# Routing head 0 of tile 0 as its own piece, with the order of TensorE, ScalarE and VectorE changed around the first row gathers

## What is computed

```python
h = h + concat([y_mla, y_diff]) @ w_out
# _peer, on n = rms_norm(h), in chunks of 128 tokens
q = (n @ w_query).reshape(128, 8, 2, 128)
s = einsum('chpd,hpnd->chpn', q, sub_keys)           # 8 heads, 2 halves, 128 keys each
s1, i1 = top_k(s[:, :, 0], 16); s2, i2 = top_k(s[:, :, 1], 16)
best, flat = top_k(all 256 sums of s1 and s2, 16)    # per head
experts = i1[flat // 16] * 128 + i2[flat % 16]       # 16 rows of 16384 for each head and token
g = softmax(best)
act = gelu(einsum('cd,chkd->chk', n, u[experts]))
h = h + einsum('chk,chkd->cd', g * act, v[experts])
```

## Time and profile before

| what | value |
| --- | --- |
| median of 3 runs | 1566.36 us |
| span of the profiled execution, first to last instruction | 1493.2 us |
| PE busy | 1221.3 us (82%) |
| DVE busy | 1039.1 us (70%) |
| POOL busy | 582.6 us (39%) |
| ACT busy | 425.9 us (29%) |
| DMA | 435.45 MB, mean 292 GB/s |

### The profile page before, as it was taken

How to read it: one execution, slowest core, us unless ns; L and a number is a source line. 1 busy time by engine, 2 the same in 40 slices (tenths; PEclk the granted TensorE clock), 3 DMA queues, 4 the chain that set the end, 5 groups by cost and what they waited for, 6 DMA issues and landing times.

```text
span 1493.2 us, 17594 instructions
## 1 busy us (share of the span) xinstructions
PE 1221.3 (82%) x6525; PEld 888.2 (59%) x6525; DVE 1039.1 (70%) x1903; ACT 425.9 (29%) x740; POOL 582.6 (39%) x644
## 2 busy tenths in 40 slices
PE   6997997677786565665566579999999999999997
PEld 3545675344443222222222229989989999899996
DVE  5786468888688775866666546677777759575655
ACT  1147213021112111211110114333345556243342
POOL 4140026777777777777777742001010000000000
PEclk9999898788998778777788899999999999999999
DMA  9917149999999999999999986888757545357651
GB/s 328 358 42 254 57 171 340 394 409 400 409 409 408 408 400 401 410 408 410 409 410 409 410 350 214 284 286 283 262 182 242 189 165 184 113 170 228 203 187 71
DMA packets 179708, 435.45 MB, mean 292 GB/s; under 512 B 13881, under 2 KB 84610, under 8 KB 179638
## 3 DMA queue, kind: packets, MB, share of 16 engines
q0 software_dynamic: 84384, 306.26, 52.3%
q1 hardware_dynamic: 94214, 126.18, 25.3%
q10 hardware_dynamic: 1040, 2.10, 0.4%
HBM read 433.44 MB, written 2.14 MB: 292 GB/s over the span
## 4 chain that ended last, share of the span: by engine, by line
PE 47%; POOL 28%; issue 10%; DVE 6%; DMA 5%; ACT 2%; SPq 0%; DVEq 0%; POOLq 0%
POOL arena L795 21%; PE quad L1505 14%; POOL ring L795 7%; PE quad_a L1610 7%; PE quad_a L1519 6%; PE quad_a L1204 4%; DMA ring<-in_ffn_w_gu_dram 3%; PE quad_a L1459 2%; PE quad_a L1305 2%; PE quad L1287 2%; DMA arena<-in_peer_v_dram,arena 2%; PE quad_a L1687 2%; PE quad_a L1675 2%; PE quad_a L1533 1%; ACT arena L823 1%
## 5 line engine op out<-in xcount | busy, mean ns | idle before, releaser
L1459 PE MATMUL quad_a<-arena 128*128 128x512 f32 x384 | 200.0, 685 | 124.0 <-DMA arena<-in_peer_v_dram,arena 124.0
L1459 PEld LDWEIGHTS quad_a<-arena 128*128 128x128 f32 x384 | 84.5, 225 | 238.9 <-issue 238.6
L795 POOL DMA_INDIRECT arena<-in_peer_v_dram,arena x193 | 186.0, 964 | 61.8 <-issue 58.0
L1505 PE MATMUL quad<-u_hi,w_hi 128*128 128x256 f32 x704 | 199.5, 283 | 0.6 <-DVE u_lo L2018 0.6
L1505 PE MATMUL quad<-u_lo,w_hi 128*128 128x256 f32 x704 | 199.2, 283 | 0.0
L1505 PE MATMUL quad<-u_hi,w_lo 128*128 128x256 f32 x704 | 199.0, 283 | 0.0
L795 POOL DMA_INDIRECT arena<-in_peer_u_dram,arena x168 | 170.9, 1017 | 58.7 <-issue 50.6
L722 POOL DMA_DIRECT2D arena<-in_w_ada_dram x60 | 31.8, 531 | 401.0 <-DVE arena L1753 398.8
L1976 DVE TENSOR_TENSOR w_lo<-ring,w_hi 128x2048 fp32r<-128x2048 f32 x66 | 150.7, 2289 | 52.2 <-ACT w_hi L994 52.0
L988 ACT ACTIVATE arena<-ident,arena 128x128 f32<-128x128 f32 x192 | 59.6, 389 | 343.4 <-DVE arena L2123 343.4
L2133 DVE SCALAR_TENSOR_TENSOR hx<-arena,hx 128x1024 f32<-128x1024 f32 x46 | 59.1, 1284 | 135.9 <-DMA arena<-in_peer_v_dram,arena 135.6
(11 more groups left out here) (374 smaller groups left out, 2415.0 us busy)
## 6 DMA issues: line engine op xcount, KB each, us to landing
ring<-in_ffn_w_gu_dram SPq DMA_DIRECT2D x44, 1024.0 KB, 9.1
arena<-in_w_ada_dram POOLq DMA_DIRECT2D x60, 512.0 KB, 6.3
ring<-in_ffn_w_down_dram SPq DMA_DIRECT2D x22, 1024.0 KB, 5.0
ring<-in_w_mix_in_dram SPq DMA_DIRECT2D x20, 1024.0 KB, 6.6
arena<-in_peer_w_query_dram SPq DMA_DIRECT2D x4, 2048.0 KB, 9.8
ring<-in_w_ada_dram POOLq DMA_DIRECT2D x12, 512.0 KB, 10.4
arena<-in_w_in_dram SPq DMA_DIRECT2D x3, 2048.0 KB, 35.7
arena<-in_w_out_dram SPq DMA_DIRECT2D x2, 2048.0 KB, 11.3
```

The lines of the kernel that those rows point to most:

```text
L795: gp.indirect_dma_start(out=rows_of(n), out_offset=None, in_=t["peer_" + kind][0], in_offset=bass.IndirectOffsetOnAxis(ap=expert[tt][:, sl ...
L1459: last = te.matmul(sum_side[tt][:, cols], diag[:, i % DIAGS], rows_of(n)[:, cols], start=(slot == pe_slots[0]), stop=(slot == pe_slots[-1] ...
L1505: last = te.matmul(psum[c][:, w * SEQ:(w + 1) * SEQ], weight[a][:, k, (c % 2) * P:(c % 2 + 1) * P], (u_hi, u_lo)[b][:, k], start=(k == 0 a ...
```

## The change

- `PIECES` splits the first piece: head 0 and head 1 are pieces 0 and 1 now. The first quarter of the queries is made, evacuated, scored and searched in two halves of two segments (`first_query`, `first_scores`, `evac_half`, `first_keys`). The second quarter moves behind tile 1's output projection, its `top_keys` into group 1 of DVE's loop, and piece 1's `pick` into group 0.
- `values(7)` on PE and its copy on DVE move behind the transposition of `hn`; the root of tile 1's attention norm moves behind the first half evacuation on ACT, and `y_turned(1)` behind the memsets on DVE.
- On ACT, gelu of group 0 stands ahead of the `ada` evacuations, and gelu of group 1 ahead of quarters 2 and 3. On PE, `query(0, 3)` and the scores of quarters 2 and 3 move behind the sums of group 0.
- The first two query tiles leave `ring`. A new tile `row8` is the buffer 8; the turn is 9 buffers at n = 0, a tenth at n = 9 (it waits for `hn_in_psum`), two more at n = 32, four at 128, four at 160: 20 in all, before 19.
- `NORM1_AT` and `QUERY1_AT` go from 1 and 2 to 2 and 3.

```diff
-        pq_at = [(ring, 0), (ring, 512), (arena, R0 + 7168), (arena, R0 + 7680)], ...
+        pq_at = [(arena, R0 + 10240), (arena, R0 + 5632), (arena, R0 + 7168), (arena, R0 + 7680)], ...
-        OPENED = {0: range(0, 11), 128: range(11, 15), 160: range(15, 19)}
+        OPENED = {0: (0, 1, 2, 3, 4, 5, 8, 6, 7), 9: (9,), 32: (10, 11), 128: range(12, 16), 160: range(16, 20)}
-        PIECES = ((0, 0, 2), (0, 2, 2), (0, 4, 4), (1, 0, 4), (1, 4, 4))
-        ROUTE_AT = {1: 1, 5: 2, 11: 3, 18: 4}
-        KEYS_AT = {3: (0, 2), 4: (0, 3), 9: (1, 0), 10: (1, 1), 14: (1, 2), 16: (1, 3)}
-        NORM1_AT, QUERY1_AT = 1, 2
+        PIECES = ((0, 0, 1), (0, 1, 1), (0, 2, 2), (0, 4, 4), (1, 0, 4), (1, 4, 4))
+        ROUTE_AT = {1: 2, 5: 3, 11: 4, 18: 5}
+        KEYS_AT = {1: (0, 1), 3: (0, 2), 4: (0, 3), 9: (1, 0), 11: (1, 1), 14: (1, 2), 16: (1, 3)}
+        NORM1_AT, QUERY1_AT = 2, 3
...
-            pool.wait_ge(a_full.sem, a_at["ps", 0, 1] + 1)
+            pool.wait_ge(a_full.sem, a_at["ps", 0, 0, 0] + 1)
...
-                elif 11 <= buffer_of[n] < 15:
+                elif 12 <= buffer_of[n] < 16:
                     pool.wait_ge(a_full.sem, a_at["pq", 1, 0] + 1)
-                elif buffer_of[n] >= 15:
+                elif buffer_of[n] >= 16:
                     pool.wait_ge(a_full.sem, a_at["pq", 1, 1] + 1)
...
+            evac_half("pq", 0)
             root(("subln", 1))
-            evac_query("pq", 0, 0)
-            evac_query("ps", 0, 0)
-            evac_query("pq", 0, 1)
-            spread_rows(0)
-            evac_query("ps", 0, 1)
-            soft(0)
-            for job in ADA_JOBS:
-                ...
+            for what, half in (("ps", 0), ("pq", 1), ("ps", 1)):
+                evac_half(what, half)
+            for piece in range(2):
+                spread_rows(piece)
+                soft(piece)
             sc_e.wait_ge(d_free.sem, len(d_jobs))
             hn_in_psum.mark(ac.activation(hn_side[0], hn[0], ACT.Copy))
-            for what, n in (("pq", 2), ("pq", 3), ("ps", 2), ("ps", 3)):
-                evac_query(what, 0, n)
+            for what in ("pq", "ps"):
+                evac_query(what, 0, 1)
...
             for group in range(QT * GROUPS):
                 gelu_group(group)
+                if group == 0:
+                    for job in ADA_JOBS:
+                        ...
+                if group == 1:
+                    for what, n in (("pq", 2), ("pq", 3), ("ps", 2), ("ps", 3)):
+                        evac_query(what, 0, n)
...
-            top_keys(0, 0)
+            first_keys(0)
             top_pairs(0)
             pick(0)
-            top_keys(0, 1)
+            first_keys(1)
+            top_pairs(1)
             for n in range(2):
                 written_out(n, 1)
             normalize(0)
-            ve.wait_ge(a_full.sem, a_at["ada", ADA_JOBS[-1]] + 1)
...
+                if group == 0:
+                    pick(1)
+                    normalize(1)
                 if group in KEYS_AT:
```

74 lines of the change are left out of this document (49 added, 25 removed).

## The result

The changed kernel takes 1587.38 us (median of 6, 1580.12 to 1588.69), the kernel before 1565.36 us beside it (median of 6, 1563.52 to 1570.63): ratio 1.0136, 95% interval 1.0118 to 1.0153. It is slower by 22 us; forecast was 1557. One thing must be known to read any number here: the trace of before with its span of 1493.2 us was taken where this kernel takes 1496 us, and the timed runs where it takes 1565; the experiments met both kinds of chip, and each is told with the time of the kernel before beside it.

What follows compares the result with a forecast made beforehand. It took the gathers to be paced by DMA bytes from about 270 us, the end set by gather 0's issue and early losses: 9.5 - 0.8 = 8.7, call it 9; 1566.4 - 9 = 1557 us, range 1548 to 1567.

Steps and rivals of the forecast that it cites:

- With the 73.2 us between span and median: Last step: 73.2 us between traced span and median time, carried through unchanged, so 1566.4 - 9 = 1557 us.
- PE doesn't stand in the way by then: Early gathers: PE's second and third quarters, `ada` and group 0 sums, done by 243, were not to delay POOL.
- Cost nothing; the cover is 5 us: n = 32 to 127: group 1's diagonals at 254.5, its first buffer wanted at 262.7; no loss.
- a further wait among n = 32 to 60: Sign against the forecast: another wait of POOL at these gathers would show it wrong; no size given.
- Slower: Rival, chance 0.08: PE at half clock holds group 1's `v` rows until 275, buffers over 15 us late; 1576 at 20 us delay.
- The clock: Cause in the slower rival: PE at 1.2 GHz makes 20 us of sums, query and scores take 40; rival's chance 0.08.
- The steps ahead of the first gather: Reordered and halved query, search and pick before gather 0: issued at 199.2 instead of 206.80, gain 7.6 us (6 to 11).
- The waits that come: POOL at n = 18 late by 3.7 us, some 2 absorbed, and at n = 29 late by 4.7 us, both behind DVE.
- Gather 30: End of the early waits: issued at 245.3 against 254.78 before, 9.5 us sooner.
- I take 0.4 at each: Buffers opened at n = 128 and 160 wait for tile 1 queries: 2.4 us late, mostly hidden, 0.4 us lost at each.
- the short routing instructions: DVE's two-operand routing among the gathers could hold up POOL, up to 5 us, 1562; rival's chance 0.04.

Runs made afterwards that it cites:

- `b_again`: The kernel before, unedited, run again: 1496.33 us, beside 1495.93 us for the kernel before (ratio 1.0005).
- `b_third`: The kernel before, unedited, run a third time: profiled run 1561.93 us, beside 1565.25 us for the kernel before.
- `a_again`: The changed kernel, unedited, run again: 1493.32 us, beside 1495.93 us for the kernel before (ratio 0.9989).
- `a_third`: The changed kernel, unedited, run a third time: 1582.65 us, beside 1565.25 us for the kernel before (ratio 1.0107).
- `e_open`: The changed kernel with new buffers joined at n = 132 and 164 instead of 128 and 160: 1573.87 us, kernel before 1565.25 (ratio 1.0056).
- `e_direct`: The changed kernel with each gather replaced by a plain transfer of 128 successive rows, same bytes: 1484.75 us, kernel before 1565.96 (ratio 0.9486).
- `e_fix`: `e_both` with ACT's evacuations of quarters 2 and 3 in group 2, behind gelu and tile 1's root: 1563.25 us, ratio 0.9975; run again 1565.40, 0.9995.
- `e_both`: `e_split` plus new buffers joined at n = 132 and 164: 1571.31 us, kernel before 1567.08 (ratio 1.0015).
- `e_split`: The changed kernel with ACT's quarter 2 and 3 evacuations behind group 1's diagonals and `query(0, 3)` in two halves: 1585.65 us, kernel before 1567.08 (ratio 1.0115).

## Why the prediction was wrong

**The failing step is the last of the sum: "With the 73.2 us between span and median".** I took 73.2 us for time around the span. In the executions here time and span lie 1.7 us apart (1588.69 and 1587.0 in the changed kernel's own, 1493.98 and 1492.3 in `b_again`). A span of 1493.2 beside a median of 1566.36 meant that the trace came from other conditions than the times, and that 68 us of waiting were missing from it (the spans of `b_third` and `b_again`, 1560.2 and 1492.3). Every price in the sum was read from a trace without them. What made the forecast's gain a loss is the next step.

**"PE doesn't stand in the way by then", and "Cost nothing; the cover is 5 us" for the diagonals of group 1.** Right for the earlier trace rows and for `a_again`; on the chips of the timed runs `query(0, 1)` and `query(0, 3)` take 20 and 17 us instead of 7.4, the diagonals come at 282 instead of 254.5, and the cover of 5 us is gone: 13.8 us at n = 44. That is the sign that the forecast named against itself, a further wait among n = 32 to 60. The rival "Slower" had this place and nearly this price ("v rows of group 1 held until 275", over 15 us late, 1576), with another cause. The clock is not it: at 247 to 267 the granted clock was 1.00 while PE ran dry. It fell at 207 to 227 (0.67) after PE had begun to run dry, and so is a part of the price, not its source: the 32 `ada` entries behind took 6.83 us in `a_third` for 4.68 in `a_again`.

**The steps ahead of the first gather** were right: 199.2 forecast, 197.58 in `a_again`, 199.73 in the changed kernel's trace; the gain is 8.3 us on one chip (`b_again` 205.92), forecast 7.6.

**The waits that come.** n = 18: 3.7 us late forecast, 5.3 measured (5.57 less 0.30). n = 29: 4.7 forecast, 4.45 measured (4.75 less 0.30). First dot product 207.6 forecast, 206.34 in `a_again`. Gather 30: 245.3 forecast, 245.8 measured, but `b_again` has it at 252.3 and not at 254.78, so it is 6.4 us sooner, not 9.5: 2.5 us of the forecast gain were the scatter between two executions of the kernel before.

**n = 128 and 160: "I take 0.4 at each".** Mis-sized. In `a_again` the lead over `b_again` falls from 7.1 (n = 127) to 5.0 (n = 128), and from 5.7 (n = 159) to 2.2 (n = 160); 3.3 are left at n = 256. So the two opens cost 3 to 4 us where I had 0.8 (`e_open` didn't run on such a chip). By the trace 2.4 us of lateness is covered, by the Trainium skill's figure (DMA: Bandwidth & Descriptors, section on the anatomy of one DMA) about 3: neither is seen. A late issue of 2.1 us (2.40 less 0.30) was paid at once, and 0.7 of it was made up by n = 159. The reason stands in the earlier trace rows, and the forecast misread it. At 420 to 460 POOL is busy for 30.62 of 40 us, and the 0.30 us between its 31 gathers are another 9.3. So POOL had no time left: it was the bound there as much as the DMA engines were, and an engine that issues without a pause has next to nothing to catch up with. `e_direct` shows how close the two bounds lie. POOL needs 0.53 us for a transfer there and has 1% of the chain that ended last, where the trace of before has 28%; the DMA engines move 409 GB/s at 420 to 460 as before, and the whole kernel takes 9 us less than `a_again` on another chip. Two slips in the sum: 425.9 less 423.67 is 2.2 us late, not 2.4, and without the late opens it gives 1556.9, not 1556.5; nothing hangs on either. Without dry time the change is worth 2.6 us by the medians (1495.93 to 1493.32), and the interval of the ratio (0.9974 to 1.0005) includes no change.

**Where the 22 us went** (by `a_third` and `b_third`): the 11.7 us won by n = 32 went by n = 44 behind a query that ran dry, and by n = 64 the changed kernel was 6.1 us behind; then 6.2 and 11.6 us at the late opens, of which some is made up. `e_fix`, with the waits at 44, 128 and 160 down to 3.2, 0.3 and 5.2 us and that at 26 still 9.1, is level. That the waits cause the loss is shown, for the opens by `e_open` and `e_both`, and for ACT's and DVE's part behind `query(0, 3)` by `e_fix`; taking away the wait at 44 alone (`e_split`) brought nothing. That late instructions cause the waits is shown by `a_again`: the same program has none of them, no wait for PE at n = 26 or 44, and shorter ones at 128 and 160. How much of it is PE's lateness and how much DVE's or ACT's isn't told apart. Why an indirect gather delays other engines' instructions, and why on some chips alone, stays open. The instruction transfers that the page lists (`q8 instruction: 41, 0.67, 0.2%`) are the same in both conditions.

**The added row and POOL**: gather 29 of `a_again` took 1.94 us beside a row of DVE with two operands in SBUF, and most others 0.94, as in the earlier trace rows. The Trainium skill (SBUF — State Buffer, section Who interferes with whom) has that; the short routing instructions cost nothing that can be seen, as forecast.

## What to carry to other kernels

Hold the profiled execution's span against the timed runs before any sum: a gap of more than a few us is not overhead but a trace from other conditions, and its waits are not those of the runs. When an engine's busy time and its fixed pauses fill a stretch, it is the bound there, though it waits for nobody. A long row of small instructions on one engine is a risk in a stretch full of indirect gathers: cut it (two halves of 32 entries ran through in `e_both`, though one of 32 ran dry in `b_third`, at 308.8 to 315.9) and don't put gelu, diagonals or evacuations that free buffers behind it. Buffers that wait for such a job join the turn when it is surely done; four gathers later brought 0.5 to 1% where the kernel before takes 1565 us; where it takes 1496 us that wasn't run.
